# The gates of one token tile: added into a cleared DRAM table by indirect transfers, in place of one-hot products

## The reference

```
q = (x wq) per head, 8 heads, two halves             # s = q . sub_keys, 128 keys per half
sv, si = top_k(s, 16)                                # per half
top, pos = top_k(sv[0][:, None] + sv[1][None, :], 16)
eidx = si[0] * 128 + si[1] at pos                    # 16 experts of 16384 per token and head
g = softmax(top)
a = gelu(u[eidx] . x)
y = sum over heads and the 16 of  g * a * v[eidx]
```

## Time and profile before

| | |
|---|---|
| median of three runs | 1540.63 us |
| the profiled execution | 1543.53 us, of it span 1541.7 |
| PE busy | 1489.7 us, 97% |
| DVE busy | 1277.7 us, 83% |
| ACT busy | 710.9 us, 46% |
| POOL busy | 617.1 us, 40% |
| mean granted clock of PE | 0.994 |

### The profile page before, as it was taken

One profiled execution on the slowest core, in us unless ns is written; L12 is line 12 of the kernel. 1 busy time (PEld: TensorE's weight loads), 2 busy tenths in 40 slices (PEclk: granted clock), 3 DMA queues, 4 the chain that ended last, 5 costly groups with the idle time before them and its releaser, 6 DMA issues.

```text
span 1541.7 us, 24351 instructions
## 1 busy us (share of the span) xinstructions
PE 1489.7 (97%) x8276; PEld 1325.4 (86%) x8276; DVE 1277.7 (83%) x2494; ACT 710.9 (46%) x1409; POOL 617.1 (40%) x508
## 2 busy tenths in 40 slices
PE   4999999999998999999899999999999999999997
PEld 4877777888898999999899999999999988888886
DVE  5788665689998979889759888889899988888787
ACT  3444553233345747567544444444444434443433
POOL 1121300033461424344246555556767655455300
PEclk9999999999999999999999999999999999999999
DMA  9754320133355888989899999999999999999962
GB/s 365 274 171 163 136 84 1 41 97 95 98 179 163 272 253 269 297 251 325 252 357 397 337 363 359 352 356 363 385 395 385 376 364 411 384 379 387 348 242 96
DMA packets 164099, 417.14 MB, mean 271 GB/s; under 512 B 12697, under 2 KB 70169, under 8 KB 163873
## 3 DMA queue, kind: packets, MB, share of 16 engines
q1 hardware_dynamic: 95936, 244.88, 44.5%
q0 software_dynamic: 41472, 151.01, 25.9%
q10 hardware_dynamic: 26594, 20.05, 4.0%
HBM read 376.57 MB, written 38.80 MB: 269 GB/s over the span
## 4 chain that ended last, share of the span: by engine, by line
PE 79%; DVE 16%; DMA 2%; ACT 2%; issue 1%; ACTq 0%; DVEq 0%; SPq 0%
PE bank_S L1061 16%; PE bank_T L1061 11%; PE bank_G L1061 5%; PE bank_T L1039 5%; PE bank_O L1001 5%; PE bank_O L1003 5%; PE bank_O L1002 5%; PE bank_S L1001 3%; PE bank_S L1003 3%; PE bank_S L1002 3%; PE bank_O L761 2%; PE bank_S L728 2%; DVE mod_acc L2221 2%; DVE mod_acc L2191 2%; DVE v_sb L2197 1%; DVE v_sb L2184 1%
## 5 line engine op out<-in xcount | busy, mean ns | idle before, releaser
L1673 ACT ACTIVATE v_hi<-v_raw 128x1024 fp32r<-128x1024 f32 x124 | 131.6, 1061 | 287.0 <-PE bank_G L1061 278.7
L1642 ACT ACTIVATE u_hi<-u_raw 128x1024 fp32r<-128x1024 f32 x128 | 135.4, 1058 | 211.5 <-PE bank_O L1003 107.3
L2465 DVE TENSOR_TENSOR v_lo<-v_raw,v_hi 128x1024 fp32r<-128x1024 f32 x124 | 152.1, 1227 | 87.8 <-ACT v_hi L1673 63.1
L1001 PE MATMUL bank_S<-h_hi,u_hi 128*128 128x352 f32 x576 | 196.3, 341 | 7.9 <-DVE u_lo L2299 2.7
L1393 POOL DMA_INDIRECT row<-in_peer_v,stage x128 | 177.0, 1383 | 42.2 <-issue 37.5
L1393 POOL DMA_INDIRECT row<-in_peer_u,stage x128 | 146.3, 1143 | 104.3 <-POOL stage L1389 99.8
L1002 PE MATMUL bank_S<-h_lo,u_hi 128*128 128x352 f32 x576 | 186.3, 323 | 0.0
L2455 DVE SCALAR_TENSOR_TENSOR y<-row,wgt,y 128x1024 f32<-128x1024 f32 x128 | 164.5, 1285 | 0.0
L2481 DVE SCALAR_TENSOR_TENSOR row<-row,h 128x1024 f32<-128x1024 f32 x128 | 156.2, 1221 | 0.0
L1001 PE MATMUL bank_O<-h_hi,u_hi 128*128 128x352 f32 x448 | 145.2, 324 | 0.0
L1002 PE MATMUL bank_O<-h_lo,u_hi 128*128 128x352 f32 x448 | 144.3, 322 | 0.0
(11 more groups left out here) (436 smaller groups left out, 3938.7 us busy)
## 6 DMA issues: line engine op xcount, KB each, us to landing
u_raw<-in_u_t SPq DMA_DIRECT2D x128, 512.0 KB
v_raw<-in_peer_v SPq DMA_DIRECT2D x128, 512.0 KB
g_in<-gates SPq DMA_DIRECT2D x32, 768.0 KB
ada_late<-in_w_ada SPq DMA_DIRECT2D x8, 2048.0 KB, 8.2
gates<-g_out SPq DMA_DIRECT2D x8, 2048.0 KB, 11.6
spill<-a_act ACTq DMA_DIRECT2D x64, 176.0 KB
a_act<-spill SPq DMA_DIRECT2D x16, 704.0 KB
w_raw<-in_w_in SPq DMA_DIRECT2D x20, 512.0 KB, 4.0
```

The source lines that it names most:

```text
L1001: pe.matmul(ps[:, 0:DX], u_hi[q][:, kk], h_hi[:, k, GT * P:S - XT], start=(k == 0), stop=False)
L1642: act.activation(u_hi[c % 2][:, :], u_raw[:, c % 2, :], ACT.Copy).then_inc(s_uhi, 1)
L1673: act.activation(v_hi_end[:, i % TAIL, :] if end else v_hi[:, c % 2, :], v_raw[c % 4][:, :], ACT.Copy)\
L2465: dve.tensor_tensor(lo[:, q, :], v_raw[c % 4][:, :], hi[:, q, :].bitcast(f32), ALU.subtract)\
```

## The change

Tile 2's blocks (4 to 7) are no longer made by products. Their part of `gates` is cleared by 16 transfers of 512 KB (8 MB) from a zero tile, which VectorE sets at step J = 30 of the attention part and SP issues behind the second load of `x`; SP waits for them ahead of the loads of `wq`. For each token and choice, six small VectorE operations (`scatter_places`) work out the place in the table, and POOL adds the gates there with 128 indirect transfers, each 128 elements of 4 bytes (one choice of each of the 128 tokens), `compute_op=ALU.add`. After every 16 of them (one head) POOL waits until all so far have landed, since two heads of a token can name one expert. They are dealt out over POOL's list by `SCAT_BESIDE`, 3 to 5 to a chunk, from chunk 32 to chunk 69, behind that chunk's `u_lo` and gathers of x. SP waits for all 128 before `load_g(0)`.

The plan of the early chunks becomes: 23 alone, blocks 8 to 10 (23 to 28), 14 alone, blocks 0 to 3 (43 to 50), 13 alone, block 11 (64, 65), 6 alone. So POOL makes `u_lo` of chunks 43 to 51 and 64 to 66 (before: 36 to 44, 50 to 58 and 64 to 66), and VectorE those in between. The decode of tile 2 moves into the first gap, ahead of that of tile 1. The dots of x move: 5 in the first gap (chunks 39 to 41), 8 in the phase, 16 at chunks 51 to 56. Waits that counted twelve blocks count eight; three semaphores of the kernel's start are merged into others.

```diff
-PHASES = [[8, 9, 10], [0, 1, 2, 3], [4, 5, 6, 7], [X_BLOCK]]
-PHASE_TILE = [3, 1, 2, 3]
-GAPS = [23, 7, 6, 6]
+SCAT_TILE = 2
+SCAT_BLOCKS = slice(4, 8)
+ZERO_PIECES = 16
+PHASES = [[8, 9, 10], [0, 1, 2, 3], [X_BLOCK]]
+PHASE_TILE = [3, 1, 3]
+GAPS = [23, 14, 13]
...
+ORDERED = len(PLACE_OF)
...
-DOTS_AFTER = {30: 1, 31: 1, 32: 1, 45: 1, 46: 1, 47: 1, 58: 3, 59: 2, 60: 2}
+DOTS_AFTER = {39: 2, 40: 2, 41: 1, 51: 2, 52: 3, 53: 3, 54: 3, 55: 3, 56: 2}
+SCAT_BESIDE = dict([(i, 3) for i in range(32, 57)] + [(i, 4) for i in range(57, 64)] + [(64, 5), (65, 5)]
+                   + [(i, 4) for i in range(66, 70)])
...
+        zeros = at("zeros", 96, [P, 512])
+        place_u = at("place_u", 62, [P, P], u32)
+        quarter_u = at("quarter_u", 62.5, [P, P], u32)
+        quarter_f = at("quarter_f", 63, [P, P])
+        place_f = at("place_f", 63.5, [P, P])
...
             sp.wait_ge(s_accd, 12)
             sp.dma_start(x_sb[:, :, :], x[0].rearrange("(t p) d -> p t d", p=P)).then_inc(s_x, 16)
+            sp.wait_ge(s_zero, 4)
+            for n in range(ZERO_PIECES):
+                step = NCHUNK // 4 // ZERO_PIECES
+                sp.dma_start(gates[:, step * n:step * n + step, SCAT_BLOCKS, :, :].rearrange("p q b i t -> p q (b i t)"),
+                             zeros[:, :].unsqueeze(1).to_broadcast([P, step, 512])).then_inc(s_cleared, 16)
             sp.wait_ge(s_inlo, 20)
...
             unit_done(sp, 19)
+            sp.wait_ge(s_cleared, 16 * ZERO_PIECES)
             for e in range(2):
                 sp.dma_start(wq_raw[:, e % 4, :], wq[e]).then_inc(s_wq[e % 4], 16)
...
-                    sp.wait_ge(s_idx, NT)
+                    sp.wait_ge(s_idx, NT - 1)
                     for m in range(4):
                         load_v(m, m, False)
                 if i == EARLY - 2:
-                    sp.wait_ge(s_gst[0], 16 * stores_of(BLOCKS - 2))
-                    sp.wait_ge(s_gst[1], 16 * stores_of(BLOCKS - 3))
+                    sp.wait_ge(s_gst[0], 16 * stores_of(ORDERED - 2))
+                    sp.wait_ge(s_gst[1], 16 * stores_of(ORDERED - 3))
                     sp.wait_ge(s_gfirst, 16)
+                    sp.wait_ge(s_scat, 16 * P)
                     load_g(0, 0, False)
...
+            pool.iota(token_at[:, :], [[0, 1]], base=(SCAT_TILE - GT) * 4 * P, channel_multiplier=1,
+                      allow_small_or_imprecise_dtypes=True).then_inc(s_const, 1)
...
+            gate_places = gates.rearrange("p q b i t -> (p q b i t)").unsqueeze(1)
+
+            def scatter(first, end):
+
+                for n in range(first, min(end, P)):
+                    if n % TOPK == 0 and n:
+                        pool.wait_ge(s_scat, 16 * n)
+                    pool.indirect_dma_start(gate_places, bass.IndirectOffsetOnAxis(place_u[:, n:n + 1], 0),
+                                            gate[:, SCAT_TILE, n:n + 1], None, compute_op=ALU.add).then_inc(s_scat, 16)
+
             pool.wait_ge(s_xidx, QUARTERS)
-            got = 2
+            got, scattered = 2, 0
             gather_x(0, got)
-            for phase, blocks in enumerate(PHASES):
-                for i in range(BESIDE[blocks[0]], BETWEEN[phase + 1].start + 1):
-                    ready = dots_before(i - 2) + X_PLACES
-                    if blocks[-1] != X_BLOCK:
-                        ready = min(ready, got + 2)
-                    gather_x(got, ready)
-                    got = max(got, ready)
+            for i in range(BESIDE[PHASES[0][0]], EARLY):
+                if i in LOW_ON_POOL:
                     split_u(i, i)
+                ready = dots_before(i - 1) + X_PLACES
+                gather_x(got, ready)
+                got = max(got, ready)
+                if i == min(SCAT_BESIDE):
+                    pool.wait_ge(s_cleared, 16 * ZERO_PIECES)
+                    pool.wait_ge(s_xidx, QUARTERS + 1)
+                scatter(scattered, scattered + SCAT_BESIDE.get(i, 0))
+                scattered += SCAT_BESIDE.get(i, 0)
             pool.wait_ge(s_xdot, XN)
-            pool.wait_ge(s_idx, NT)
+            pool.wait_ge(s_idx, NT - 1)
             for n in range(3):
                 gather(n, n)
...
-                    if phase == len(PHASES) - 2 and n == len(gap) - 4:
+                    if phase == len(PHASES) - 2 and n == len(gap) - 6:
...
+                if J == 30:
+                    dve.wait_ge(s_accd, 12)
+                    dve.memset(zeros[:, :], 0.0).then_inc(s_zero, 1)
...
+            def scatter_places():
+
+                i_key, j_key = key_f[:, SCAT_TILE, 0, :], key_f[:, SCAT_TILE, 1, :]
+                done(dve, dve.tensor_copy(quarter_u[:, :], i_key), s_dv)
+                done(dve, dve.scalar_tensor_tensor(out=place_f[:, :], in0=j_key, scalar=float(NKEYS // 4 * 4 * DT),
+                                                   in1=token_at[:, :].to_broadcast([P, P]), op0=ALU.mult, op1=ALU.add),
+                     s_dv)
+                done(dve, dve.tensor_scalar(quarter_u[:, :], quarter_u[:, :], 2, None, ALU.logical_shift_right), s_dv)
+                done(dve, dve.scalar_tensor_tensor(out=place_f[:, :], in0=i_key, scalar=float(GB), in1=place_f[:, :],
+                                                   op0=ALU.mult, op1=ALU.add), s_dv)
+                done(dve, dve.tensor_copy(quarter_f[:, :], quarter_u[:, :]), s_dv)
+                dve.scalar_tensor_tensor(out=place_u[:, :], in0=quarter_f[:, :], scalar=float(4 * (DT - GB)),
+                                         in1=place_f[:, :], op0=ALU.mult, op1=ALU.add).then_inc(s_xidx, 1)
...
-                        for n in rest[0:2]:
+                        for n in rest[0:6]:
                             split_and_dot(n)
-                        rest = rest[2:]
+                        rest = rest[6:]
                         decode(0, s_idx, [(rest[0:1], [], rest[1:2]), ([], rest[2:3] + [None], [])])
                         rest = rest[3:]
                     else:
+                        decode(SCAT_TILE, s_dv, [([], rest[0:1], []), ([rest[1]], [], rest[2:3])])
+                        scatter_places()
+                        rest = rest[3:]
                         decode(phase, s_idx, [([], rest[0:1], rest[1:2]), ([], rest[2:3], rest[3:4])])
                         rest = rest[4:]
```

More of the change, by code:

```diff
@@ L312, in peer_block_kernel @@
         cand = mod_acc[:, 1, 0:2 * CAND].rearrange("p (h c) -> p h c", c=CAND)
+        token_at = sb("token_at", [P, 1])
         gsum = sb("gsum", [P, NT * PH])
@@ L338, in peer_block_kernel @@
         s_x, s_out = sem("x_loaded"), sem("out_stored")
-        s_c, s_n1, s_lam, s_small = sem("c_loaded"), sem("norm1_loaded"), sem("lam_loaded"), sem("rows_loaded")
+        s_c, s_n1, s_small = sem("c_loaded"), sem("norm1_loaded"), sem("rows_loaded")
+        s_cleared, s_scat = sem("gates_cleared"), sem("gates_scattered")
         s_b, s_n2 = sem("first_biases_loaded"), sem("norm2_loaded")
-        s_silu, s_rs, s_zero = sem("silu_ready"), sem("first_rstd_ready"), sem("bias_places_cleared")
+        s_silu, s_rs, s_zero = sem("silu_ready"), sem("first_rstd_ready"), sem("places_cleared")
         s_ada = [sem(f"ada_loaded{n}") for n in range(9)]
@@ L358, in peer_block_kernel @@
         s_pv = sem("pv_done")
-        s_sso, s_so, s_power = sem("o_squares"), sem("o_std"), sem("exponent_made")
+        s_sso, s_so = sem("o_squares"), sem("o_std")
         s_x1, s_h2 = sem("x1_ready"), sem("h2_ready")
@@ L366, in peer_block_kernel @@
         s_got_x = [sem(f"x_row_got{j}") for j in range(X_PLACES)]
-        s_hx, s_xidx, s_xdot = sem("h2_of_x_copied"), sem("x_experts_ready"), sem("x_dots")
+        s_hx, s_xidx, s_xdot = sem("h2_of_x_copied"), sem("row_places_ready"), sem("x_dots")
         s_xgelu, s_xgate = sem("x_gelus"), sem("x_gates_ready")
@@ L1047, in _ @@
             emptied(("cols", len(PHASES) - 1))
-            pe.wait_ge(s_gt, DT // 4)
+            pe.wait_ge(s_gt, len(GROUPS_IN_ORDER))
             pe.wait_ge(s_gelu, EARLY)
@@ L1291, in _ @@
             load_g(1, 1, False)
-            sp.wait_ge(s_gst[1], 16 * stores_of(BLOCKS - 1))
+            sp.wait_ge(s_gst[1], 16 * stores_of(ORDERED - 1))
             def loads(m, c, late, _):
@@ L1315, in _ @@
             pool.memset(b_half[:, :, :], 0.0).then_inc(s_zero, 1)
-            pool.memset(power[:, :], -0.5).then_inc(s_power, 1)
+            pool.memset(power[:, :], -0.5).then_inc(s_zero, 1)
             pool.memset(ident[:, :], 0.0).then_inc(s_const, 1)
@@ L1344, in _ @@
                 win_low(n)
-            pool.wait_ge(s_power, 1)
+            pool.wait_ge(s_zero, 3)
             pool.wait_ge(s_sso, 1)
@@ L1424, in _ @@
             pool.wait_ge(s_g[0], 16)
-            pool.wait_ge(s_gst[1], 16 * stores_of(BLOCKS - 1))
+            pool.wait_ge(s_gst[1], 16 * stores_of(ORDERED - 1))
             for n in range(3, RING - 2):
@@ L1441, in _ @@
             act.dma_start(lam_in[:, :, :].rearrange("p a b -> p (a b)"), lam_vecs.partition_broadcast(P))\
```

(18 more changed lines are left out.)

2 lines of the change are left out of this document (1 added, 1 removed).

## The result

The changed kernel takes **1654.8 us** (median of four executions), the kernel before on the same chip 1540.7: ratio 1.073, 95% interval 1.071 to 1.075. The forecast was 1564. The profiled execution has a span of 1648.9 us in place of 1541.7, 107.2 more.

The account below looks back on a forecast made before the run. TensorE (PE) was taken to bound the early part, but after the change POOL's 239.0 us list delays the main loop by 23.5 us: 1543.5 + 23.5 = 1567.0, less 2.9 to the median, 1564 us; range 1512 to 1604.

Parts of the forecast that it names:

- PE's work, 32.4 us: Early part, chunks 48 to 58: PE loses 32.4 us of work, the gain if all new work is hidden.
- everything costed at nothing: Early part: the clears (19 us, done at 196), DVE's splits and places were taken as hidden, cost 0.
- rival 4: Kernel's start: the clears hold up the loads of `w_outs`, up to 10 us on top; chance 1 in 6.
- The places, forecast for 562.8: First gap: DVE finishes `scatter_places` at 562.8, when POOL's list begins.
- POOL's list in order sets the end: Early part: POOL does not idle, its list sums to 239.0 us, the last scatter issued at 801.8.
- I take 1.25, the row nearest in kind: POOL's list: a scatter's step priced like a gather of x, 1.25 us, 160.0 us for 128.
- The upper bound, 1.68: POOL's list: a scatter's step at most that of the main loop's gathers of `v`, 1.38 and 0.30 us.
- Rival 3: POOL's scatters: the addition makes entries costlier, 1619 us, or additions land late, 1593; chance 0.17.
- rival 1: POOL's scatters: cheap at 0.95 us a step, landing in 2 us, groups' time kept, about 1524 us; chance 0.28.
- The other terms of the list: POOL's list: 23 gathers of x 28.8 us, 12 splits 28.8, 7 landing waits 21.4.
- The prediction's count of 43 scatters for chunks 51 to 63: Chunks 51 to 63: POOL has 43 scatters and 12 gathers in some 50 us of PE's time.
- The end, 19.4 us from the last issue to `v_chunk`: End of early part: last landing at 804.8, gates' issue, load of u, splits, two chunks; first `v_chunk` at 821.2.

Follow-up runs that it names:

- e2: Changed kernel without its 128 scatters and SP's wait for them; clears, decoding and places stay: 1512.3 us.
- e11: The kernel of e2 with the table cleared twice, the second pass after the first has landed: 1528.9 us.
- e5: Changed kernel with SP's wait for the scatters and the first load of gates behind the loads of chunks 71 and 72 of u: 1640.6 us.
- e6: Changed kernel with POOL's splits of chunks 43 to 51 and 64 to 66 on DVE: 1633.1 us.
- e7: Changed kernel with all 128 scatters on partitions 0 to 63 only, the other tokens' additions left out: 1633.7 us.
- e10: e8 with the scatters spread otherwise, 64 instead of 101 of them ahead of chunk 57: 1607.3 us.
- e3: Changed kernel with plain writes in place of the scatters' additions: 1583.2 us.
- e8: Changed kernel with tile 2 decoded ahead of the first phase, scatters begun there, e5's order on SP and e6's splits: 1605.4 us.
- e1: The probe: kernel before, with POOL issuing extra additions, plain writes and reads behind its last gather; additions cost 0.6 to 0.7 us more an instruction.
- e12: e10 with plain writes in place of additions: 1576.0 us.

## Why the prediction was wrong

By its steps:

- **PE's work, 32.4 us, and everything costed at nothing**: nearly right. Without the scatters the main loop starts 29.7 us sooner, and 28.4 are gained (e2). The clears take SP's queue 19.9 us (19 forecast) and show no cost (e11), and the splits on DVE show none either; rival 4 fell. The places, forecast for 562.8, are written at 562.5 to 562.8, and the first scatter starts at 563.6.
- **The mechanism, POOL's list in order sets the end**: right. From 563.6 to 883.7 POOL stands only for landings and for 0.6 us of DVE's dots. It reaches the split of chunk 43 at 637.4 and not at 616.4, so PE stands 34.0 us there (its longest wait) where 10 were forecast, and 31.0 at chunk 64, and the dots at 52 to 56 wait for rows; e5, e6 and e7 move the time by what they take off the list or behind it, whatever they do to the waits, and e10, with PE's earlier waits nearly gone, doesn't move it.
- **The step that failed: "I take 1.25, the row nearest in kind"**, the price of a scatter, 160.0 us for 128. It is 1.90, 243.6 us, 83.6 more. The row nearest in kind was the same instruction without the one thing that was new about it, the addition. In the probe an addition costs 0.6 to 0.7 us over a plain write or read. The kernel without it takes 1583 (e3).
- **The upper bound, 1.68**, was too low as well. It was the dearest row of the kernel before, but a row without addition; nothing in that trace bounded an addition from above, and the range should have said so. Rival 3 named the right cause with two thirds of its size (its 55 us more gave 1619), but put it on the entries; the probe puts most of it on the instruction. What spoke for rival 1 ("in no row does the issue of a gather depend on anything but the 128 entries, and these are shorter") is also refuted: shorter entries save nothing (0.97 us for 4 bytes and for 4 KB), and with additions even their number counts for little, 1.32 us at 32 and 1.68 at 128.
- The other terms of the list: gathers 29.6 forecast as 28.8; 12 splits took 35.5 for 28.8, but began under the end of a scatter, so the 6.7 don't add up; landing waits 17.5 for 21.4 (1.3 to 4.3 us each, 2.5 on average). The Trainium skill, "DMA: Bandwidth & Descriptors", section "Anatomy of one DMA — SWDGE (gpsimd) path", gives about 2.0 us as the fixed part of such a transfer, by which, as an estimate, the seven waits would have been 7.3. The traces don't agree: 2.5 us behind an issue of 1.6 make 4.1 here, and the probe has 4.5 (1.54 + 3.00). With 0.6 for DVE's dots the sum is 83.6 + 0.8 - 3.9 + 0.6 = 81.1, by which the list is longer (320.1 for 239.0). The prediction's count of 43 scatters for chunks 51 to 63 is a slip (`SCAT_BESIDE` has 46) that enters no sum.
- **The end, 19.4 us from the last issue to `v_chunk`**: 21.3. The last scatter landed 1.4 us after its issue (3.0 forecast), the load of `u` took 6.6 for 5.75, and the two chunks with what lies between took 10.4 for 7.7, the first at PE's lower clock. 81.1 + 0.8 (start) + 1.9 = 83.8, and 821.2 + 83.8 = 905.0.

## A version that beats both?

None was found. To be even, the list must end by about 789 (8.6 us ahead of the main loop, e5). The additions alone need 128 x 1.9 = 243 us of it, gathers and splits some 50, landings 16 to 28; begun at 525 they end at 837 (e8), and PE's time saved is at most 28 us (e2) for these 243 of POOL. Even without any landing wait that list would end near 821, an estimate from e8 (837.0 - 15.6). One instruction that takes the 16 columns of a head at once would change that; in every run here an instruction carries one place per partition, and no other form was tried. Nor was it tried to pack two heads of 64 tokens into one transfer: a token's equal experts of two heads could then stand in one transfer, and no run shows that both would be added. The kernel before stays the fastest that computes the whole; e2 is faster only because it leaves a third of the table out.

## What to carry to other kernels

Before work is moved to an engine that is at 40%, write its list in order and price every entry by the very form that will be issued: the same instruction with one option more (an addition instead of a write) is another instruction, and if no row shows it, the range must be open upwards, or a probe of six instructions must close it. When an engine's list sets the end, the waits of the others tell where they meet it and not what it costs: taking one away moves it on (of the 83 us at POOL's splits 54 came up at DVE's in e6; in e10 65.8 us stand in a single wait). What pays is a shorter list, so fewer instructions, not smaller ones.

## What the runs showed of the hardware

- An indirect transfer with addition holds POOL 1.57 to 1.68 us, a plain one 0.96 to 0.98, for 4 bytes and for 4 KB a partition nearly alike; an addition on 64 partitions holds it 1.42, on 32 1.32 (means of three to six in e1). The next starts 0.30 later in all cases.
- From the end of its issue to the landing 3.0 us pass for an addition on 128 partitions, 1.6 on 64 and 1.5 on 32; 3.1 for a plain write, 1.7 for a read (e1, nearly idle chip). In the changed kernel it is 1.3 to 4.3 for additions.
- A split of POOL is shown with 2.92 to 2.98 us behind an addition (after) and with 2.38 to 2.40 on average behind plain writes (e3, e12). It starts some 0.55 us before the end of the addition's issue, so of its 2.92 us here only 2.38 lie behind the addition:
```profile
636.42 1.55 POOL L1441 DMA_INDIRECT gates<-gate,place_u  x1 [1.85 <-DMA gates<-gate,place_u]
637.43 2.92 POOL L1401 TENSOR_TENSOR h_lo<-u_raw,u_hi 128x1024 fp32r<-128x1024 f32 x1
```
- PE's clock. The granted clock was 0.79 and 0.78 in the windows in which PE stood longest (34.0 and 31.0 us in one piece). After the stand of 18.6 us the first chunk began at the lower of the two levels (1.2 GHz) and went back to the upper (2.4) some 4.5 us later:
```profile
894.75 0.63 PE L1017 MATMUL bank_S<-h_hi,u_hi 128*128 128x352 f32 x1 [18.63 <-DVE h_lo L2343]
895.18 0.49 PE L1018 MATMUL bank_S<-h_lo,u_hi 128*128 128x352 f32 x1
...
899.45 0.32 PE L1018 MATMUL bank_S<-h_lo,u_hi 128*128 128x352 f32 x1
```
- The waits of the kernels with plain scatters that no queue in the profile explains (e3, e12), left open above.
